# Gated linear attention: outputs summed in PSUM over both directions, state updates scaled by ScalarE, heads normalised in two halves

## What is computed

```python
# GLA recurrence S_t = diag(a_t) S_{t-1} + k_t^T v_t, o_t = q_t S_t, in chunks of 64
o_f, s_f = scan(q, k, v, log_a_f, s0);  o_b, s_b = scan(flip(q, k, v), flip(log_a_b), s0)
o = o_f + flip(o_b)
y = o * rsqrt(mean(o * o, over the 96 of a head) + 1e-6) * norm_g
out = y * silu(gate)
```

## Time and profile before

| | us |
|---|---|
| median of 3 runs | 2648.06 |
| lowest, highest | 2647.53, 2664.75 |
| the profiled execution | 2677.43 |
| its span in the trace | 2675.6 |
| TensorE busy in the span | 2373.2 |
| VectorE busy | 1394.8 |
| ScalarE busy | 589.8 |
| GpSimd busy | 1105.0 |

### The profile page before, as it was taken

One profiled execution on the slowest core, in us unless ns is written; L12 is line 12 of the kernel. 1 busy time (PEld: TensorE's weight loads), 2 busy tenths in 40 slices (PEclk: granted clock), 3 DMA queues, 4 the chain that ended last, 5 costly groups with the idle time before them and its releaser, 6 DMA issues.

```text
span 2675.6 us, 34115 instructions
## 1 busy us (share of the span) xinstructions
PE 2373.2 (89%) x14068; PEld 1901.7 (71%) x14068; DVE 1394.8 (52%) x2005; ACT 589.8 (22%) x1159; POOL 1105.0 (41%) x632
## 2 busy tenths in 40 slices
PE   7998799999799996999996989559688896899998
PEld 5866588887577774888883657448487895688886
DVE  4455657456733346474466430777945554550431
ACT  2052220121232222210211300302533221210110
POOL 4613367666342232667662204404110024456663
PEclk9999899999899998999996999769789768899999
DMA  4201125335121111334354101102010001222321
GB/s 154 95 24 48 48 95 176 108 103 193 48 71 40 40 45 42 102 136 143 101 173 178 38 3 58 54 1 80 31 49 3 2 1 55 66 92 95 106 91 63
DMA packets 54058, 204.12 MB, mean 76 GB/s; under 512 B 6000, under 2 KB 6128, under 8 KB 52880
## 3 DMA queue, kind: packets, MB, share of 16 engines
q1 hardware_dynamic: 52560, 188.34, 21.5%
q0 software_dynamic: 1344, 13.60, 1.3%
HBM read 197.72 MB, written 4.19 MB: 75 GB/s over the span
## 4 chain that ended last, share of the span: by engine, by line
PE 81%; DVE 14%; ACT 3%; issue 1%; POOL 1%; DMA 0%; DVEq 0%; SPq 0%; POOLq 0%; ACTq 0%
PE bank L493 59%; PE bank L781 3%; PE bank L809 2%; PE bank L610 1%; DVE nb L619 1%; PE bank L1359 1%; PE bank L1367 1%; PE bank L1339 1%; PE bank L2022 1%; PE bank L796 1%; DVE nb L1911 1%; PE bank L2277 1%; PE bank L2018 1%; PE bank L785 1%; DVE big L1902 1%
## 5 line engine op out<-in xcount | busy, mean ns | idle before, releaser
L493 PE MATMUL bank<-xn_r,parts_r 128*128 128x512 f32 (+1 forms) x3104 | 975.3, 393 | 48.1 <-DVE big_r L504 13.3
L493 PE MATMUL bank<-big_r,parts_r 128*128 128x512 f32 x3112 | 898.2, 392 | 1.0 <-POOL parts_r L484 1.0
L482 POOL TENSOR_SCALAR parts_r<-ring 128x1024 fp32r<-128x1024 f32 x297 | 337.1, 1135 | 1182.3 <-PE bank L493 1157.7
L484 POOL TENSOR_TENSOR parts_r<-ring,parts_r 128x1024 fp32r<-128x1024 f32 x297 | 743.3, 2503 | 24.8
L493 PEld LDWEIGHTS bank<-xn_r,parts_r 128*128 128x128 f32 x3104 | 589.1, 192 | 174.9 <-issue 41.6
L493 PEld LDWEIGHTS bank<-big_r,parts_r 128*128 128x128 f32 x3112 | 583.4, 189 | 123.4 <-DVE big_r L504 2.7
L740 DVE SCALAR_TENSOR_TENSOR big<-bank,small,big 128x511 f32<-128x511 f32 x88 | 65.9, 749 | 268.1 <-ACT big L719 268.1
L719 ACT ACTIVATE big<-bank,small 128x512 f32<-128x512 f32 x88 | 68.3, 781 | 488.3 <-PE bank L493 488.3
L2418 DVE TENSOR_TENSOR big<-big 128x512 f32<-128x512 f32 x32 | 82.2, 2573 | 70.5 <-ACT big_r L2399 70.5
L2372 DVE SCALAR_TENSOR_TENSOR h<-bank,vecs,h 128x512 f32<-128x512 f32 x24 | 17.8, 750 | 193.4 <-PE bank L493 193.4
L493 PE MATMUL bank<-parts_r,xn_r 128*128 128x384 f32 x352 | 95.2, 353 | 15.5 <-DVE big L1902 9.6
(11 more groups left out here) (348 smaller groups left out, 3004.3 us busy)
## 6 DMA issues: line engine op xcount, KB each, us to landing
ring<-weights SPq DMA_DIRECT2D x297, 512.0 KB, 3.5
cst<-mod_w SPq DMA_DIRECT2D x48, 512.0 KB, 4.0
big<-consts POOLq DMA_DIRECT2D x1, 4096.0 KB, 15.9
cst<-consts SPq DMA_DIRECT2D x2, 1280.0 KB, 8.4
h<-x SPq DMA_DIRECT2D x8, 256.0 KB, 5.2
h_store<-h POOLq DMA_DIRECT2D x1, 2048.0 KB, 7.7
h<-h_store POOLq DMA_DIRECT2D x1, 2048.0 KB, 9.0
out<-mix SPq DMA_DIRECT2D x8, 256.0 KB, 2.2
```

The lines of the kernel that those rows point to most:

```text
L482: pool.tensor_scalar(rounded(w_hi[:, slot]), w, 1.0, 0.0, ALU.mult, ALU.add).then_inc(sem("hi_ready"), 1)
L484: pool.tensor_tensor(rounded(w_lo[:, slot]), w, value(w_hi[:, slot]), ALU.subtract).then_inc(part_ready, 1)
L493: mm = pe.matmul(ps, rounded(w[a]), rounded(x[b]), start=(start and n == 0), stop=(stop and n == 2))
```

## The change

- Banks 4 to 7 hold the outputs for the whole stage. `inner` writes the first sums there, and the scan's query products (`cross`) add to them in PSUM with `start=False`, both directions into the same place. A pair of token blocks shares two banks: blocks 1 and 2 in banks 4 and 5 (complete after n = 9), blocks 0 and 3 in banks 6 and 7 (complete after n = 11). `gl_o`, its copies (L1680) and its sums (L1713) are gone.
- Keys are turned through banks 2 and 3.
- ScalarE scales `U` out of PSUM to one of two buffers, four instructions of 128x96 for a step. VectorE updates the state by four `scalar_tensor_tensor` of 128x96 for a step (state times decay plus scaled `U`). The last step's update, which nobody reads, is left out, and the first is a copy. TensorE makes `U` two steps ahead. `gl_Sr` has two buffers.
- The close: for each pair of blocks ScalarE squares the two banks, VectorE reduces, scales, ScalarE takes the root, VectorE the reciprocal, two multiplications out of PSUM and one by the gate. GpSimd has multiplied the gate by `norm_g` beforehand, between its splits of `gl_g` and of `gd_q`.

The diff without the shared semaphore tables (which only rename counts: `gl_u` 11 and `gl_S` 11 new, `gl_in` gone, `gla_ss` and `gla_sd` 2) and without most deleted lines:

```diff
-        gl_U = part(18064, 4, GLA_DV)
-        gl_o = mix[:, 2:5].rearrange("p k t -> p (k t)").rearrange("p (b n) -> p b n", b=TB)
+        gl_U = [part(a, 4, GLA_DV) for a in (18064, 18448)]
+        OUTS = ((1, 2), (0, 3))
+        def gl_out(tb, hd, rows_=slice(0, P)):
+            p, t = out_of[tb]
+            at_ = (2 * t + hd // 2) * GLA_DV
+            return bank[4 + 2 * p + hd % 2][rows_, at_:at_ + GLA_DV]
@@ gla_pe
-                ps = grab(pe, 4 + tb % 2, *after("gl_in", tb + 1))
                 for hd in range(GH):
-                    mm = pe.matmul(ps[:, hd * GLA_DV:(hd + 1) * GLA_DV], gl_A[:, tb % 2, hd * P:(hd + 1) * P],
-                                   gl_v[:, CB + tb, hd * GLA_DV:(hd + 1) * GLA_DV], start=True, stop=True)
+                    mm = pe.matmul(gl_out(tb, hd), gl_A[:, tb % 2, hd * P:(hd + 1) * P],
+                                   gl_v[:, CB + tb, hd * GLA_DV:(hd + 1) * GLA_DV],
+                                   start=(hd < 2 and tb in (OUTS[0][0], OUTS[1][0])), stop=False)
+            def cross(n):
+                for d in range(2):
+                    ...
+                    pe.wait_ge(sem("gl_Sr"), 2 * (n - CCH) + d + 1)
+                    for hd in (0, 2, 1, 3):
+                        q, dc = 64 * (hd % 2), 2 * d + hd // 2
+                        mm = pe.matmul(gl_out(c // 2, hd, slice(r, r + CH)), gl_q1[q:q + 64, dc, c * CH:(c + 1) * CH],
+                                       gl_Sr[(n - CCH) % 2][q:q + 64, dc, :], start=False,
+                                       stop=(hd >= 2 and n in last_cross))
+                    mm.then_inc(sem("gl_x"), 1)
+            update(0)
+            update(1)
+            for n in range(NCH):
+                if n >= CCH:
+                    cross(n)
+                if n + 2 < NCH - 1:
+                    update(n + 2)
@@ gla_act
+            for n in range(NCH - 1):
+                act.wait_ge(*after("gl_U", n + 1))
+                if n >= 2:
+                    act.wait_ge(*after("gl_S", n - 1))
+                for dc in range(4):
+                    c = steps(dc // 2)[n]
+                    ins = act.activation(gl_U[n % 2][:, dc], bank[2 * (n % 2) + dc // 2][:, (dc % 2) * GLA_DV:(dc % 2 + 1) * GLA_DV],
+                                         ACT.Copy, scale=gl_sc[:, 2, dc * NCH + c:dc * NCH + c + 1])
+                ins.then_inc(sem("gl_u"), 1)
@@ gla_dve
-                dve.wait_ge(*after("gl_o", tb + 1))
-                dve.tensor_copy(gl_o[:, tb], bank[4 + tb % 2][:, 0:GW]).then_inc(sem("gl_in"), 1)
+                m = n - CCH
+                if m >= 0:
+                    if m >= 2:
+                        dve.wait_ge(*after("gl_x", 2 * m - 2))
+                    for d in range(2):
+                        dve.tensor_tensor(gl_Sr[m % 2][:, 2 * d:2 * d + 2], gl_S[:, 2 * d:2 * d + 2],
+                                          scol(0, d, steps(d)[n]), ALU.mult).then_inc(sem("gl_Sr"), 1)
+                if n == NCH - 1:
+                    break
+                dve.wait_ge(*after("gl_u", n + 1))
+                ...
+                    for dc in range(4):
+                        c = steps(dc // 2)[n]
+                        ins = dve.scalar_tensor_tensor(out=gl_S[:, dc], in0=gl_S[:, dc],
+                                                       scalar=gl_sc[:, 1, dc * NCH + c:dc * NCH + c + 1],
+                                                       in1=gl_U[n % 2][:, dc], op0=ALU.mult, op1=ALU.add)
+        def gla_gate_pool(pool):
+            pool.wait_ge(*after("gla_gate", TB))
+            pool.tensor_tensor(g, g, small_cols("gla_ng", GLA_DV).unsqueeze(1).broadcast_to((P, 4 * TB, GLA_DV)), ALU.mult)\
+                .then_inc(sem("gla_gate_scaled"), 1)
+        def gla_close_act(act):
+            for p in range(2):
+                act.wait_ge(*after("gl_x", 2 * (last_cross[p] - CCH + 1)))
+                if p == 0:
+                    act.activation(stat[:, 16:17], gain("eps"), ACT.Sqrt)
+                for hh in range(2):
+                    act.activation(gl_sqr[:, 2 * p + hh], bank[4 + 2 * p + hh][:, 0:GW], ACT.Square).then_inc(sem("gla_squared"), 1)
+                act.wait_ge(*after("gla_ss", p + 1))
+                act.activation(stat[:, 8 * p:8 * p + 8], stat[:, 8 * p:8 * p + 8], ACT.Sqrt).then_inc(sem("gla_sd"), 1)
@@ block2_pool
-            split_units(pool, UNITS["gl_q"], UNITS["gd_k"])
+            split_units(pool, UNITS["gl_q"], UNITS["gd_q"])
+            gla_gate_pool(pool)
+            split_units(pool, UNITS["gd_q"], UNITS["gd_k"])
```

More of the change, by code:

```diff
@@ L1597, in steps @@
             return list(range(NCH)) if d == 0 else list(range(CCH))[::-1] + list(range(CCH, NCH))[::-1]
+        last_cross = [CCH + max(2 * max(pair) + 1, 2 * TB - 1 - 2 * min(pair)) for pair in OUTS]
         def gla_pe(pe):
@@ L1696, in gla_dve @@
-                for d in range(2):
-                    c = steps(d)[n]
-                    S, u = gl_S[:, 2 * d:2 * d + 2], gl_U[:, 2 * d:2 * d + 2]
-                    dve.tensor_tensor(S, S, scol(1, d, c), ALU.mult)
-                    U = bank[2 * (n % 2) + d][:, 0:2 * GLA_DV].rearrange("p (a n) -> p a n", a=2)
-                    ins = dve.tensor_tensor(u, U, scol(2, d, c), ALU.mult)
-                ins.then_inc(sem("gl_Su"), 1)
-                dve.wait_ge(*after("gl_Su", n + 1))
-                link(dve, dve.tensor_tensor(gl_S[:, :], gl_S[:, :], gl_U[:, :], ALU.add))
@@ L1705, in gla_dve @@
-                if n >= CCH:
-                    for d in range(2):
-                        c = steps(d)[n] - CCH
-                        r = CH * (c % 2)
-                        dve.wait_ge(*after("gl_x", 2 * (n - CCH) + d + 1))
-                        for hh in range(2):
-                            o = v4(gl_o[r:r + CH, c // 2])[:, hh::2]
-                            x_ = bank[4 + 2 * d + hh][r:r + CH, 0:2 * GLA_DV].rearrange("p (a n) -> p a n", a=2)
-                            dve.tensor_tensor(o, o, x_, ALU.add).then_inc(sem("gl_add"), 1)
-                        dve.wait_ge(*after("gl_add", 4 * (n - CCH) + 2 * d + 2))
+                        dve.tensor_tensor(gl_Sr[m % 2][:, 2 * d:2 * d + 2], gl_S[:, 2 * d:2 * d + 2],
+                                          scol(0, d, steps(d)[n]), ALU.mult).then_inc(sem("gl_Sr"), 1)
@@ new lines, in gla_dve @@
+                dve.wait_ge(*after("gl_S", n + 1))
+        def gla_gate_pool(pool):
+            g = gate.rearrange("p b (h n) -> p (b h) n", h=GH)
+            pool.wait_ge(*after("gla_gate", TB))
[10 more added lines that the diff above has]
+                act.activation(stat[:, 8 * p:8 * p + 8], stat[:, 8 * p:8 * p + 8], ACT.Sqrt).then_inc(sem("gla_sd"), 1)
+            for c in range(3):
+                act.wait_ge(*after("gla_flip", c + 1))
+                act.activation(mix[:, 2 + c], bank[4 + c % 2][:, :], ACT.Copy).then_inc(sem("gla_cat"), 1)
@@ new lines, in gla_close_dve @@
+        def gla_close_dve(dve):
+            t4 = lambda a: a.rearrange("p (t h n) -> p t h n", t=2, h=2)
+            by_head = gl_res.rearrange("p b (a h n) -> p b a h n", a=2, h=2)
+            for p, (first_, last_) in enumerate(OUTS):
+                s8 = stat[:, 8 * p:8 * p + 8]
+                for hh in range(2):
+                    dve.wait_ge(sem("gla_squared"), 2 * p + hh + 1)
+                    ins = dve.tensor_reduce(s8[:, 4 * hh:4 * hh + 4], gl_sqr[:, 2 * p + hh].rearrange("p (q n) -> p q n", q=4),
+                                            AX.X, ALU.add)
+                link(dve, ins)
+                dve.tensor_scalar(s8, s8, 1.0 / GLA_DV, EPS, ALU.mult, ALU.add).then_inc(sem("gla_ss"), 1)
+                dve.wait_ge(*after("gla_sd", p + 1))
+                link(dve, dve.reciprocal(s8, s8))
+                two = slice(first_, last_ + 1, last_ - first_)
+                for hh in range(2):
+                    ins = dve.tensor_tensor(by_head[:, two, :, hh], t4(bank[4 + 2 * p + hh][:, 0:GW]),
+                                            s8[:, 4 * hh:4 * hh + 4].rearrange("p (t h) -> p t h", t=2).unsqueeze(3)
+                                            .broadcast_to((P, 2, 2, GLA_DV)), ALU.mult)
+                link(dve, ins)
+                if p == 0:
+                    dve.wait_ge(sem("gla_gate_scaled"), 1)
+                ins = dve.tensor_tensor(gl_res[:, two], gl_res[:, two], gate[:, two], ALU.mult)
+            ins.then_inc(sem("gla_normed"), 1)
```

75 lines of the change are left out of this document (33 added, 42 removed).

## The result

The changed kernel took 2638.36 us (median of 17 runs, 2624.51 to 2671.34), the kernel before, in as many runs beside it, 2664.75 (2647.53 to 2687.29). The ratio is 0.9896 with a 95% interval of 0.987 to 0.9922; it leaves out two slow executions of the changed kernel (2669.15 and 2671.34 us, at granted clocks of 0.920 and 0.919), which the medians include. By this ratio the change makes the kernel 27.7 us faster, 21 to 35; the medians differ by 26.4. Its 2625.3 over 2648.06 is a ratio of 0.9914. The median of 2638.36 itself lies 0.4 us above its range; the measured ratio times 2648.06 is 2620.5, inside it.

The account below looks back on a forecast made before the run. VectorE was taken to bound the stage. Gains of 3.7 (blocks), 20.5 (scan) and 2.3 (close) less a 3.7 loss (GpSimd) give 22.8 us, taking 2648.06 to 2625.3 us; range 2612 to 2638.

Parts of the forecast that it names:

- What bounds: Whole stage: VectorE sets the pace, so what shortens the stage shortens the kernel unless a later stage waits; 22.8 us.
- the 37.7 named as a sign: Expected length in us from the first masks to the heads' last multiplication, if the forecast is right.
- (b): The four token blocks: VectorE's wait for the product and its copy vanish, TensorE is late next; gain 3.7 us.
- (c): The scan: steps from n = 4 on take 1.71 us on VectorE instead of 3.81; gain 20.5 us.
- (a): Decays, queries and keys: moved GpSimd work frees the decays (5.7) but delays queries and keys (9.4); loss 3.7 us.
- the clock only as a gain: Part of the rival that more comes out (0.27): TensorE, idle less, keeps its high clock into the stage's end; 1 to 2 us.
- the prediction's estimate from that page: Scan: with four updates at 0.64 us, the loop over the engines would bind at 1.52 a step; 1.3 us more gain.
- the rival that the loop over the engines binds: Scan: the path across engines, not VectorE, sets the step at 2.1 us; gain only 17.7 us, kernel 2630; chance 0.15.
- (d): Close of the heads: two halves, ScalarE's squares covered by other work, 7.4 us instead of 9.67; gain 2.3 us.
- The other side: Scan: adding in PSUM serialises the cross products, eight steps lose 40 us, kernel 2665; chance 0.04.
- Within 1%: Whole kernel: a change of no more than 1% either way, given 0.64, against 0.33 for faster by over 1%.

Follow-up runs that it names:

- gate_after_splits: Changed kernel with GpSimd's first two gd_q splits back in their old place and the gate's product after them; 2653.59 us, one run.
- gate_late: Changed kernel with GpSimd's gate product and first gd_q splits held until VectorE has scaled the keys; 2628.57 us, ratio 0.9886 to the kernel before.
- pe_busy: Changed kernel with TensorE multiplying unread constants into bank 6 while it waits for the keys; 2630.62 us, ratio 0.9873 to the kernel before.
- close_whole: Changed kernel with the heads normalised in one piece after the last cross product instead of in two halves; 2658.25 us, one run.
- both: Changed kernel with the late gate product and splits plus constant matmuls (20 + 1 + 1 + 1) ahead of the blocks; 2631.53 us, ratio 0.9883 to the kernel before.
- both_shorter: Changed kernel with the late gate product and splits plus fewer constant matmuls (15 + 1 + 1); 2625.19 us, ratio 0.9865 to the kernel before.

## Why the prediction was right, and where not

- **What bounds.** Right. All that the change does shows between the first decay scan and the last multiplication by the gate, VectorE sets the pace of the scan from n = 4 on, and no later stage shows a sizeable new wait. The stage lost 19.9 us of the 22.8 predicted. From the first masks to the heads' last multiplication it is 42.2 us instead of the 37.7 named as a sign: 3.5 of the difference is (b), 1.1 is (c).
- **(a) GpSimd.** Right in mechanism and nearly in size: 5.6 gained, 8.7 lost, a loss of 3.1 instead of 3.7. The term that was off is the gate's product, 2.94 us instead of 3.6: 1.9 ns a column, where the undisturbed L484 takes 2.3. That the splits cost the same beside keys as beside decays is shown by `gate_after_splits` (39.7 and 40.0 us); that the whole is avoidable by `gate_late`.
- **(b) Token blocks.** The step that failed. The working took the 1.71 us of the scores from the earlier trace rows for every block. VectorE's wait and copy did go, and TensorE is late next, as said; but it ran at 1.2 GHz from the third block's scores on, with 2.99 and 3.09 for them, and gave back 3.5 of the 3.7. `pe_busy` shows that it was the clock: with it at 1.00 the blocks take 9.84, within 0.1 of what the working gives (1754.25 - 1744.31 = 9.94). All seven traces that have the new blocks and no constants show it, with 13.0 to 13.6 us. A duration that comes from a stretch at the high clock holds only as long as that clock does, and the prediction named the clock only as a gain and held that nothing in the stage scales with it. That gain came too, ahead of the blocks: the transposes and first scores, for which the sum had no term, took 1.0 less.
- **(c) Scan.** Right: 19.4 instead of 20.5. Four updates take 1.00 us (1.02 predicted), each 313 ns by the mean of its line (320 predicted). A step is 1.77 instead of 1.71, since 0.10 and not 0.03 lies between `gl_Sr` and the first update: 0.4 over seven steps. The start took 8.44 instead of 7.65, and 7.20 at the high clock: that part is (b)'s error again. The Trainium skill, page "VectorE: DVE Perf Modes", section "The TRN2 errata", has a row by which the four would take 0.64, the prediction's estimate from that page; the trace has 1.00, so the row of wider instructions was the better guide, and the rival that the loop over the engines binds did not come.
- **(d) Close.** Right: 7.31 instead of 7.4, and the cover of ScalarE's squares is worth the 0.9 that the prediction gave it (`close_whole`).
- **The other side.** Adding in PSUM serialises nothing here: at the low clock 14 records of L1657 take 1.02 us, as 14 of L1655, which did not add, did before. Sixteen take 1.18 at the low clock and 0.82 at the high one, and the step has no wait for them.
- **The step to the whole.** The sum was set against 2648.06, the median of three runs; seventeen gave 2664.75. The ratio predicted, 0.9914, lies in the first two intervals and under the third. "Within 1%", the likelier call, holds by the ratios of two comparisons (0.9921 and 0.9966) and just misses by that of the first (0.9896). How near the whole came to the forecast is in part luck: 7.8 us of the first comparison's 27.7 are not in the stage, and in the third 11 us of the stage's gain do not appear.

Left open: why the clock fell in the blocks of the changed kernel. In both traces TensorE idled for 26 to 29 us and began the transposes at 1.2 GHz. In the changed kernel the clock rose at 1739.6, 3.1 us after the first transpose, and fell at 1746.5; in the kernel before it rose at 1742.9, 6.1 after the first transpose, and fell only at 1756.6, after the last scores. Between rise and fall TensorE idled for no more than 1.3 us at a time in either. `both` kept the clock and `both_shorter` did not, with six constants fewer. No run separates what decides between them.

## What to carry to other kernels

Where VectorE and GpSimd take turns, moving the work of one helps only if it lands beside nothing of that kind: ask for each place what the other engine then does with two SBUF inputs. When a wait of VectorE goes, and TensorE is late next, price TensorE's part at both of its clocks. And where the whole kernel scatters by more than the change, read the stage by a start and an end that both kernels have.

## What the runs showed that was not expected

- The same 49 matmul records of the later blocks met a granted clock of 0.93 before the change and 0.51 after it, and kept TensorE busy 5.61 us of 10.38 and 9.91 of 10.14. Much of the second figure is the low clock itself: at 1.00 (`pe_busy`) all four blocks are 7.60 busy of 9.84.
- Constants multiplied into a free bank ahead of a dense stretch kept it at 1.00 and paid 3.6 us in the blocks and 1.2 at the scan's start; ended earlier, they shortened the transposes and let the clock fall later instead.
- VectorE and GpSimd took turns so strictly that four splits beside the decays or beside queries and keys cost VectorE the same: 39.7 or 40.0 us for the path.
- The comparisons of the same two kernels on three occasions gave 28, 21 and 9 us with intervals of 7 to 11 us either way, at stages that differ by 1 us.
